# GLA layer of a two-block kernel: the gate's low-rank products stacked into one pass and moved, identity transposes put at the start, weight splits and boundary steps put in another order

## The chip, the cores and the metric

One core of a Trainium2 chip. The time is the device time of one launch in microseconds (us), the median of several runs. The profile is one more execution, recorded by the hardware profiler.

## What is computed

Two blocks run one after the other on x [256, 1024]. The first has a GLA mixer, a feed-forward (FFN), an attention mixer and a second FFN; the second has a recurrent mixer (`lru`) and a short-convolution mixer (`sc`). The change lies in the GLA mixer and in the steps between layers. Cut to what matters:

```python
h = rmsnorm(x, norm_mix[0])
proj = h @ w_in                                  # q, k: 512 columns each; v, g: 1024 each; r: 32
q, k, v, g, r = jnp.split(proj, [...], axis=-1)
r_f, r_b = jnp.split(r, 2, axis=-1)              # 16 columns a direction
def log_decay(r_dir, w_up, b_up):                # w_up [16, 512]
    return log_sigmoid(r_dir @ w_up + b_up) / 16.0
la_f, la_b = log_decay(r_f, ...), log_decay(r_b, ...)
o = gla_chunked(q, k, v, la_f, strict=False) + flip(gla_chunked(flip(q), flip(k), flip(v), flip(la_b), strict=True))
x = x + (rmsnorm(o, gla_norm) * silu(g)) @ w_out
x = x + conv_ffn(rmsnorm(x, norm_ffn[0]), ...)   # then attention, a second FFN, and the second block
```

## The kernel before

It is written engine by engine: each of the five engines has its own program, in a fixed order, and waits on semaphores. Nothing reorders anything, so an instruction that waits holds all that stands behind it on its engine.

**Weights** come as a stream of units of 128x2048 f32 (1 MB). SyncE loads unit u into one of three raw buffers; ScalarE writes its rounded high part `w_hi` (`split(u)`, L426); VectorE subtracts to get the low part `w_lo` (`split(u)`, L732), which also frees the raw buffer, so that SyncE may load unit u+3. High and low parts live in rings of six slots. A product of full precision is three passes of TensorE in the f32r format: high by high, high by low, low by high. Units 0 and 1 are q, 2 and 3 k, 4 to 7 v, 8 to 11 g, 12 to 15 the output projection, 16 on the FFN. `wide` (L1277) makes a turned result [columns, 256 positions], 48 matmuls of 256 columns a unit; `tall` (L1290) a result [positions, 1024] in `acc`, 24 matmuls of 512 columns a unit.

**Start.** x is loaded in two tiles of 128 positions. ScalarE squares and sums, GpSimd makes `rstd`, VectorE scales (`xn`, L740), TensorE turns `xn` by transposes against `ident` (L1224, eight of 128x128 a tile), which GpSimd makes after three other fills. Out of the turned tiles come `h_hi` (for the first half of tile 0 on VectorE, `front`, L746; for the other 12 blocks on ScalarE, `high`, L441) and `h_lo` (`low`, L758, eight on VectorE).

**The gate.** `wr` [1024, 32] is split into `wr_hi` and `wr_lo`, and 24 matmuls give r turned in 32 rows (L1319). VectorE copies them to `rt` (L820). After q and k, TensorE multiplies `gup` [32, 2, 512] by `rt` in plain f32, eight matmuls of 256 columns on 32 rows (L1330) into four ring banks; this is z. ScalarE takes |z + b| (L488), an exponential and a logarithm, VectorE min(z + b, 0) (L861), a subtraction (L871) and eight scans (L875). `differences`, the exponentials and `products` of a head follow (L884, L892 to L904), and TensorE's `scores(0)` waits for them. Between k and `scores(0)` TensorE has v (`project(U_V)`). VectorE also works out the constants `lam` of the recurrent mixer there (L824 to L845, some 25 tiny operations).

**The turn and the FFN behind it.** The GLA output is normed, turned (`turn`), and multiplied by units 12 to 15, tile 0 whole and then tile 1. When tile 0 is done, `residual(…, 0)` adds it to x, and x is normed and turned for `ffn0`, while TensorE is at tile 1; then the same for tile 1. VectorE's and ScalarE's splits 16 to 20 stand between these steps.

**Boundaries** ahead of `mix1`, `ffn1`, `lru` and `sc`: four halves of `residual` (L784), the sums of squares on ScalarE, the norm, the turn. VectorE norms the first half of tile 0 ahead of the last residual half.

Of the kernel before, what the change touches and what calls it, by code (L numbers as in the profile page):

```python
# [9 lines left out]
P = 128  # L10
D = 1024
S = 256
# [55 lines left out]
def generations():  # L68
# [3 lines left out]
    stages = [("rank", 1, 1), ("q", 2, 0), ("k", 2, 0), ("z", 4, 4),  # L72
# [51 lines left out]
HI = 1 + KC  # L124
LO = KC
N_CONSTS = 3
# [30 lines left out]
def two_block_kernel(nc, x_in, stream, par_in, row_in, wr_in, gup_in, gatew_in, rope_in, out):  # L157
# [4 lines left out]
    with ctx:  # L162
# [22 lines left out]
        gup = put("gup", [2 * GLA_RANK, 2, GLA_KEYS])  # L185
# [5 lines left out]
        rt = put("rt", [2 * GLA_RANK, S])  # L191
# [24 lines left out]
        wr_hi = put("wr_hi", [P, KC, 2 * GLA_RANK], f32r, at=stage_at)  # L216
        wr_lo = put("wr_lo", [P, KC, 2 * GLA_RANK], f32r, at=stage_at + 4 * KC * 2 * GLA_RANK)
# [33 lines left out]
        half_added = sem("half_added")  # L251
        wr_hi_ready, wr_lo_ready = sem("wr_hi_ready"), sem("wr_lo_ready")
# [10 lines left out]
        xn_ready = sem("xn_ready")  # L263
        x_turned = sem("x_turned")
# [5 lines left out]
        tables_ready = sem("tables_ready")  # L270
        z_abs, soft_ready, scan_ready = sem("z_abs"), sem("soft_ready"), sem("scan_ready")
# [31 lines left out]

        block = ctx.enter_context(nc.Block())
# [3 lines left out]
        def _(sp):  # L308
# [35 lines left out]
        def _(pool):  # L344
            own = Chain(pool, pool_own)
            own.mark(nc.gpsimd.memset(power[:, :], -0.5))
            for b in (ident, causal, chunk_on):
                own.mark(nc.gpsimd.memset(b[:, :] if b is not causal else b[:, :, :], 1.0))
            own.wait()
            nc.gpsimd.affine_select(out=ident[:, :], in_=ident[:, :], compare_op=ALU.is_equal, fill=0.0,  # L350
                                    base=0, pattern=[[-1, P]], channel_multiplier=1).then_inc(made, 1)
            nc.gpsimd.affine_select(out=causal[:, :, :], in_=causal[:, :, :], compare_op=ALU.is_ge, fill=0.0,
# [64 lines left out]
        def _(act):  # L417
# [10 lines left out]
            def sums(t, name):  # L428

                for half in range(2):  # L430
# [38 lines left out]
            nc.scalar.activation(wr_hi[:, :, :], wr[:, :, :], ACT.Copy).then_inc(wr_hi_ready, 1)  # L469
            turned0("mix0")  # L470
            turned1("mix0")
            split(0)
            split(1)

            own.mark(nc.scalar.activation(lam_p[:, :], par[:, C_LAM:C_LAM + LRU_HEADS], ACT.Abs))
            own.wait()
            nc.scalar.activation(lam_e[:, :], lam_p[:, :], ACT.Exp, scale=-1.0).then_inc(lam_ready, 1)
            for u in range(2, 6):
                split(u)

            for d in range(2):
                for b in range(2):
                    g = GEN["z"] + 2 * d + b
                    act.wait_ge(filled, FULL["z"] + 2 * d + b)
                    for k in range(2):
                        h = 2 * b + k
                        c = C_GB + GLA_HEADS * d + h
                        last = nc.scalar.activation(lt[:, d, h, :], ring[:, g % 4, k * S:(k + 1) * S], ACT.Abs,  # L488
                                                    bias=par[:, c:c + 1])
                        own.mark(last) if k == 0 else last.then_inc(z_abs, 1)  # L490
                split(6 + d)
# [7 lines left out]
            split(8)  # L499
# [18 lines left out]
            split(13)  # L518
            split(14)
# [3 lines left out]
            split(15)  # L523
# [8 lines left out]
            turned0("turn")  # L532
            turned1("turn")
            split(16)
            split(17)
# [189 lines left out]
        def _(dve):  # L725
# [9 lines left out]
            def normed(name, t, half):  # L735

                if half == 0:
                    dve.wait_ge(rms_ready, RMS[name] + t + 1)
# [3 lines left out]
            def front(name):  # L742

                c = C_GAMMA[name]
                dve.wait_ge(x_turned, HALVES * NTH[name] + 1)
                nc.vector.tensor_tensor(h_hi[:, 0:4, 0:P], turned_at(name, 0, 0, 4).rearrange("p (k s) -> p k s", k=4),  # L746
# [953 lines left out]
```

## Time and profile before

| | |
|---|---|
| median of 3 runs | 928.17 us (925.98 to 928.79) |
| the profiled execution, its own time | 925.22 us |
| its span | 923.5 us |
| TensorE matmuls | 880.2 us busy, 95% of the span |
| VectorE, ScalarE, GpSimd | 628.6, 500.8, 34.2 us busy |
| mean granted TensorE clock | 0.986 |

The span is what the trace covers; the time of the same execution is 1.7 us longer. The granted clock is TensorE's, as a share of 2.4 GHz, so 0.50 is 1.2 GHz. A busy time counts overlapping instructions once.

### The profile page before, as it was taken

Reading aid. Unit: us, or ns where it says so; the run is one execution under the profiler, and the core shown is the slowest. Engines: PE = TensorE matmul, PEld = TensorE weight load, DVE = VectorE, ACT = ScalarE, POOL = GpSimd, SP = SyncE. Lnnn points to the kernel's source line nnn. Section 1 sums busy time; section 2 is a strip of 40 time slices with the busy share of each in tenths; the row PEclk is TensorE's granted clock in tenths of the full one; section 3 lists DMA queues with packets and bytes.
Section 4 is the critical chain, followed back from the end, with each engine's and each line's share of the span. In section 5 each row is a group of like instructions: output and inputs, shape, how many; then the busy total and the mean of one; then the engine's idle time right before and its main releaser. Section 6 shows DMA issues by size and latency. Waiting matters only on the chain.

```text
span 923.5 us, 15067 instructions
## 1 busy us (share of the span) xinstructions
PE 880.2 (95%) x5804; PEld 802.6 (87%) x5804; DVE 628.6 (68%) x849; ACT 500.8 (54%) x675; POOL 34.2 (4%) x76
## 2 busy tenths in 40 slices
PE   6999988999999999799999999999999899999996
PEld 5988778999999977577999999979999789999995
DVE  5798656867667678766776676758877675654643
ACT  6466454645555453465564544548988674353431
POOL 2000100000000022101000000000000000000001
PEclk9999998999999999799999999999999999999999
DMA  8443433564554515135555355336264035545421
GB/s 321 174 162 137 182 137 137 185 227 144 219 182 165 215 48 210 46 137 178 210 202 208 136 222 187 143 131 229 97 227 178 24 125 218 204 159 205 166 85 45
DMA packets 22346, 152.52 MB, mean 165 GB/s; under 512 B 2496, under 2 KB 2624, under 8 KB 5024
## 3 DMA queue, kind: packets, MB, share of 16 engines
q1 hardware_dynamic: 21936, 149.45, 44.0%
q0 software_dynamic: 368, 2.49, 0.7%
q8 instruction: 29, 0.48, 0.2%
q14 instruction: 13, 0.11, 0.0%
HBM read 150.88 MB, written 1.05 MB: 165 GB/s over the span
## 4 chain that ended last, share of the span: by engine, by line
PE 85%; DVE 6%; ACT 5%; POOL 1%; issue 1%; DMA 0%; POOLq 0%; ACTq 0%; DVEq 0%
PE ring L1277 49%; PE acc L1290 26%; PE ring L1255 2%; DVE w_lo L732 1%; ACT xn L435 1%; PE acc L1224 1%; PE ring L1537 1%; PE acc L1452 1%; PE ring L1261 1%; PE ring L1488 1%; DVE x L784 1%; PE acc L1512 1%; ACT w_hi L426 1%; ACT h_hi L441 1%; POOL rstd L375 1%
## 5 line engine op out<-in xcount | busy, mean ns | idle before, releaser
L732 DVE TENSOR_TENSOR w_lo<-raw,w_hi 128x2048 fp32r<-128x2048 f32 (+1 forms) x146 | 317.7, 2199 | 101.9 <-ACT w_hi L426 101.7
L1277 PE MATMUL ring<-h_hi,w_hi 128*128 128x256 f32 x1280 | 363.5, 284 | 0.1
L1277 PE MATMUL ring<-h_hi,w_lo 128*128 128x256 f32 x1280 | 362.4, 283 | 0.0
L1277 PE MATMUL ring<-h_lo,w_hi 128*128 128x256 f32 x1280 | 362.4, 283 | 0.0
L426 ACT ACTIVATE w_hi<-raw 128x2048 fp32r<-128x2048 f32 (+1 forms) x146 | 264.2, 1841 | 14.2 <-DMA raw<-in_stream_dram 12.8
L1277 PEld LDWEIGHTS ring<-h_hi,w_hi 128*128 128x128 f32 x1280 | 243.9, 191 | 1.7 <-DVE w_lo L732 0.3
L1277 PEld LDWEIGHTS ring<-h_lo,w_hi 128*128 128x128 f32 x1280 | 243.9, 191 | 1.5
L1277 PEld LDWEIGHTS ring<-h_hi,w_lo 128*128 128x128 f32 x1280 | 243.9, 191 | 0.0
L972 DVE SCALAR_TENSOR_TENSOR cacc<-ring,par,cacc 128x255 f32<-128x255 f32 x176 | 76.9, 478 | 51.3 <-ACT cacc L546 46.3
L1290 PE MATMUL acc<-w_hi,a_hi 128*128 128x512 f32 x272 | 107.8, 396 | 3.9 <-DVE a_lo L1149 2.6
L1290 PE MATMUL acc<-w_hi,a_lo 128*128 128x512 f32 x272 | 107.5, 395 | 0.0
L1290 PE MATMUL acc<-w_lo,a_hi 128*128 128x512 f32 x272 | 107.0, 393 | 0.0
L546 ACT ACTIVATE cacc<-ring,par 128x256 f32<-128x256 f32 x88 | 44.9, 559 | 104.5 <-PE ring L1277 98.5
L1290 PEld LDWEIGHTS acc<-w_hi,a_hi 128*128 128x128 f32 x272 | 51.5, 189 | 15.3 <-DVE a_lo L1149 3.0
L1290 PEld LDWEIGHTS acc<-w_hi,a_lo 128*128 128x128 f32 x272 | 51.5, 189 | 11.2
L1290 PEld LDWEIGHTS acc<-w_lo,a_hi 128*128 128x128 f32 x272 | 51.5, 189 | 10.1
L1290 PE MATMUL acc<-w_hi,h_hi 128*128 128x512 f32 x128 | 51.3, 400 | 1.6 <-DVE h_lo L1083 0.9
L1290 PE MATMUL acc<-w_hi,h_lo 128*128 128x512 f32 x128 | 50.3, 393 | 0.0
L1290 PE MATMUL acc<-w_lo,h_hi 128*128 128x512 f32 x128 | 50.3, 393 | 0.0
L556 ACT ACTIVATE sgl<-cacc 128x512 f32<-128x512 f32 x22 | 13.9, 632 | 47.6 <-DVE cacc L972 47.6
L696 ACT ACTIVATE sgs<-ring 128x256 f32<-128x256 f32 x12 | 4.6, 384 | 62.2 <-PE ring L1277 62.2
L435 ACT ACTIVATE xn<-x 128x512 f32<-128x512 f32 x28 | 17.6, 629 | 33.9 <-DVE x L784 31.8
(205 smaller groups left out, 858.5 us busy)
## 6 DMA issues: line engine op xcount, KB each, us to landing
raw<-in_stream_dram SPq DMA_DIRECT2D x134, 1024.0 KB, 4.8
raw<-in_stream_dram SPq DMA_DIRECT2D x12, 512.0 KB, 5.2
gatew<-in_gatew_dram POOLq DMA_DIRECT2D x1, 1536.0 KB, 6.9
x<-in_x_dram SPq DMA_DIRECT2D x2, 512.0 KB, 3.8
out_dram<-xn SPq DMA_DIRECT2D x2, 512.0 KB, 2.6
row<-in_row_dram POOLq DMA_DIRECT2D x1, 640.0 KB, 8.7
par<-in_par_dram SPq DMA_DIRECT2D x1, 274.0 KB, 4.5
rope<-in_rope_dram POOLq DMA_DIRECT2D x1, 256.0 KB, 8.5
```

The costliest lines, as they stand in the source:

```text
L375: nc.gpsimd.tensor_tensor(rstd[:, t:t + 1], mean[:, t:t + 1], power[:, t:t + 1], ALU.pow).then_inc(rms_ready, 1)
L426: nc.scalar.activation(w_hi[:, u % RING, 0:n], raw[:, u % RAW, 0:n], ACT.Copy).then_inc(hi_split, 1)
L435: nc.scalar.activation(xn[:, t, at], x[:, t, at], ACT.Square, scale=D ** -0.5, accum_out=stat[:, 2 * t + half:2 * t + half + 1]).then_inc( ...
L441: return nc.scalar.activation(h_hi[:, kc, t * P:(t + 1) * P], turned_at(name, t, kc), ACT.Copy, scale=par[:, c:c + 1])
L546: last = nc.scalar.activation(cacc[:, k, half, :], ring[:, (G + 2 * e + k) % 4, half * S:(half + 1) * S], ACT.Identity, scale=par[:, bass. ...
L556: nc.scalar.activation(sgl[:, :, :], cacc[:, :, 1, :], ACT.Silu).then_inc(gate_ready, 1)
L732: nc.vector.tensor_tensor(w_lo[:, u % RING, 0:n], raw[:, u % RAW, 0:n], w_hi[:, u % RING, 0:n].bitcast(f32), ALU.subtract).then_inc(lo_spl ...
L784: nc.vector.tensor_tensor(x[:, t, at], acc[:, t, at], x[:, t, at], ALU.add).then_inc((half_added, acc_free[t])[half], 1)
L972: last = nc.vector.scalar_tensor_tensor(out=cacc[:, k, half, out_at], in0=ring[:, bank, lo + in_at.start:lo + in_at.stop], scalar=par[:, b ...
L1255: nc.tensor.matmul(ring[:, b, f * S:(f + 1) * S], w_parts[a][:, u % RING, lo:lo + P], h_hi[:, kc, :], start=kc == 0 and f == 0 and a == 0, ...
L1277: last = nc.tensor.matmul(ring[:, b, f * S:(f + 1) * S], w_parts[a][:, slot, lo:lo + P], h_parts[c][:, kc, :], start=kc == 0 and n == 0, s ...
L1290: last = nc.tensor.matmul(acc[:, t, half * 512:(half + 1) * 512], lhs(a, kc, t), w_parts[c][:, slot, j * D + half * 512:j * D + (half + 1) ...
```

## The change

1. GpSimd makes `ident` first, and TensorE multiplies it by itself 36 times (`WARM`) while x loads.
2. `wr_hi` and `wr_lo` hold three copies of the 32 columns, so that the 24 gate matmuls give r in 96 rows. `rt` gets rows 0 to 31 high, 32 to 63 low, 64 to 95 high; `gup` is loaded three times (behind unit 0), and holds high, high, low. Eight f32r matmuls on 96 rows then give all three parts of z at once. They stand behind the second q unit and write to `acc`; v waits for `z_read`. The first q unit is `first_wide`.
3. In the start VectorE makes the first half of `h_hi` of both tiles, and ScalarE eight blocks.
4. Evictions of q and k, splits and `lam` stand in another order; splits 16 and 17 are made ahead of and within the turn, and TensorE turns tile 0 for `ffn0` one unit earlier.
5. At the four boundaries ScalarE norms the first half of tile 0 (`xn_front`), and VectorE makes the last two residual halves back to back.

```diff
@@ constants @@
-HI = 1 + KC
+HI = {n: (1 + KC) * i - (KC // 2 if i else 0) for i, n in enumerate(NORMS)}
+WARM = 36
-N_CONSTS = 3
+N_CONSTS = 2
+COPIES = 3
+RANKS = COPIES * 2 * GLA_RANK
@@ sync @@
-            sp.dma_start(gup[:, :, :], gup_in.rearrange("r (a n) -> r a n", a=2)).then_inc(consts_loaded, 16)
-            for u in range(RAW):
-                load(u)
+            load(0)
+            for c in range(COPIES):
+                sp.dma_start(gup_raw[c * 2 * GLA_RANK:(c + 1) * 2 * GLA_RANK, :, :],
+                             gup_in.rearrange("r (a n) -> r a n", a=2)).then_inc(gup_loaded, 16)
+            load(1)
+            load(2)
@@ scalar: boundary @@
-                for t in range(T):
-                    sums(t, name)
+                sums(0, name)
+                sums(1, name, (0,))
+                act.wait_ge(rms_ready, RMS[name] + 1)
+                act.wait_ge(sumsq, SUMS[name] + 1)
+                nc.scalar.activation(xn[:, 0, 0:512], x[:, 0, 0:512], ACT.Copy, scale=rstd[:, 0:1]).then_inc(xn_front, 1)
+                sums(1, name, (1,))
@@ scalar: around the turn @@
-            split(15)
+            split(16)
...
             turned0("turn")
+            split(17)
             turned1("turn")
-            split(16)
-            split(17)
@@ vector: boundary @@
-                residual(layer, units, 1, (0,))
-                normed(name, 0, 0)
-                residual(layer, units, 1, (1,))
+                residual(layer, units, 1)
@@ vector: start @@
-            front("mix0")
+            for t in range(T):
+                front("mix0", t)
             low("mix0")
             split(0)
             split(1)
             dve.wait_ge(filled, FULL["rank"])
-            nc.vector.tensor_copy(rt[:, :], ring[0:2 * GLA_RANK, GEN["rank"] % 4, 0:S]).then_inc(ring_free, 1)
+            lower = slice(2 * GLA_RANK, 4 * GLA_RANK)
+            own.mark(nc.vector.tensor_copy(rt[:, :], ring[0:RANKS, GEN["rank"] % 4, 0:S]))
+            own.wait()
+            nc.vector.tensor_tensor(rt[lower, :], ring[lower, GEN["rank"] % 4, 0:S], rt[lower, :].bitcast(f32),
+                                    ALU.subtract).then_inc(ring_free, 1)
+            dve.wait_ge(gup_hi_ready, 1)
+            lower = slice(4 * GLA_RANK, RANKS)
+            nc.vector.tensor_tensor(gup[lower, :, :], gup_raw[lower, :, :], gup[lower, :, :].bitcast(f32),
+                                    ALU.subtract).then_inc(gup_ready, 1)
@@ tensor @@
-            pe.wait_ge(made, 3)
+            pe.wait_ge(made, 1)
+            for _ in range(WARM):
+                nc.tensor.transpose(ring[:, 3, 0:P], ident[:, :], ident[:, :])
...
-            for u, g in ((U_Q, GEN["q"]), (U_Q + 1, GEN["q"] + 1), (U_K, GEN["k"]), (U_K + 1, GEN["k"] + 1)):
-                wide(u, g % 4, g=g)
-            for d in range(2):
-                for b in range(2):
...
+            for n in range(4):
+                if n == 0:
+                    first_wide("mix0", U_Q, GEN["q"] % 4)
+                else:
+                    wide(U_Q + n, (GEN["q"] + n) % 4, g=GEN["q"] + n)
+                if n == 1:
+                    pe.wait_ge(gup_ready, 1)
+                    for d in range(2):
+                        for h in range(GLA_HEADS):
+                            last = nc.tensor.matmul(z_of(d, h), gup[:, d, h * P:(h + 1) * P], rt[:, :],
+                                                    start=True, stop=True, skip_group_check=True)
...
+            pe.wait_ge(z_read, 4)
             project(U_V)
...
-                    if (t, n) == (1, 3):
+                    if (t, n) == (1, 2):
                         turn("ffn0", 0)
```

TensorE's program from the gate to v, before (L1277 k's last unit, L1330 z, L1290 v's first):

```order
L1277 MATMUL ring<-h_lo,w_hi 128x256
L1277 MATMUL ring<-h_hi,w_lo 128x256
L1330 MATMUL ring<-rt,gup 128x256 x8
L1290 MATMUL acc<-w_hi,h_hi 128x512
L1290 MATMUL acc<-w_lo,h_hi 128x512
```

and in the change, where L1368 is the 36 identity transposes, L1280 the turn of x, L1379 the gate products, L1335 the q and k units and L1391 z:

```order
L1368 MATMUL ring<-ident 128x128 x36
L1280 MATMUL acc<-ident,xn 128x128 x16
L1379 MATMUL ring<-h_hi,wr_hi 96x256
...
L1335 MATMUL ring<-h_lo,w_hi 128x256
L1335 MATMUL ring<-h_hi,w_lo 128x256
L1391 MATMUL acc<-rt,gup 128x256 x8
L1335 MATMUL ring<-h_hi,w_hi 128x256
```

z has moved from behind k to between the second q unit and the first k unit, and its matmuls now write to `acc`.

VectorE's program from the second q eviction to the first `products` (L892, in the change L936), before (L732 is a split, `qT` and `kT` are evictions of q and k, L861 reads z):

```order
L848 TENSOR_SCALAR qT<-ring 128x512 x2
L732 TENSOR_TENSOR w_lo<-raw,w_hi 128x2048
L853 COPY kT<-ring 128x512 x2
L732 TENSOR_TENSOR w_lo<-raw,w_hi 128x2048
L861 TENSOR_SCALAR la<-ring,par 128x256 x4
L732 TENSOR_TENSOR w_lo<-raw,w_hi 128x2048
L861 TENSOR_SCALAR la<-ring,par 128x256 x4
L732 TENSOR_TENSOR w_lo<-raw,w_hi 128x2048
L871 TENSOR_TENSOR lt<-la,lt 128x1024
L875 SCALAR_TENSOR_TENSOR la<-chunk_on,lt 128x256 x4
L884 TENSOR_TENSOR dd<-la 128x256 x2
L732 TENSOR_TENSOR w_lo<-raw,w_hi 128x2048
```

and in the change (L761 is a split):

```order
L863 TENSOR_SCALAR qT<-ring 128x512
L879 TENSOR_SCALAR la<-acc,par 128x256 x8
L867 COPY kT<-ring 128x512
L761 TENSOR_TENSOR w_lo<-raw,w_hi 128x2048
L884 TENSOR_SCALAR lam_q<-lam_e 128x12
...
L761 TENSOR_TENSOR w_lo<-raw,w_hi 128x2048
L867 COPY kT<-ring 128x512
L761 TENSOR_TENSOR w_lo<-raw,w_hi 128x2048
L915 TENSOR_TENSOR lt<-la,lt 128x1024
L919 SCALAR_TENSOR_TENSOR la<-chunk_on,lt 128x256 x4
L761 TENSOR_TENSOR w_lo<-raw,w_hi 128x2048
```

The reading of z (`la`) now stands ahead of the k evictions and of splits 4 to 8, `lam` (the first of its rows is L884) behind split 4, and split 7 behind the scans.

VectorE's program around the turn, before (L938 norms the GLA output, L771 is `low_of`, L784 `residual`, L740 the norm of x):

```order
L771 SCALAR_TENSOR_TENSOR h_lo<-ring,par,h_hi 128x128 x4
L938 SCALAR_TENSOR_TENSOR xn<-acc,rstd,sg 128x256 x4
L771 SCALAR_TENSOR_TENSOR h_lo<-ring,par,h_hi 128x128 x12
L732 TENSOR_TENSOR w_lo<-raw,w_hi 128x2048 x2
L784 TENSOR_TENSOR x<-acc,x 128x512 x2
L740 TENSOR_SCALAR xn<-x,rstd 128x512 x2
L732 TENSOR_TENSOR w_lo<-raw,w_hi 128x2048
L746 TENSOR_TENSOR h_hi<-acc,par 128x4x128
L732 TENSOR_TENSOR w_lo<-raw,w_hi 128x2048
L784 TENSOR_TENSOR x<-acc,x 128x512 x2
```

and in the change (L984, L801, L814, L768 are the same four):

```order
L801 SCALAR_TENSOR_TENSOR h_lo<-ring,par,h_hi 128x128 x4
L984 SCALAR_TENSOR_TENSOR xn<-acc,rstd,sg 128x256 x4
L801 SCALAR_TENSOR_TENSOR h_lo<-ring,par,h_hi 128x128 x4
L761 TENSOR_TENSOR w_lo<-raw,w_hi 128x2048
L801 SCALAR_TENSOR_TENSOR h_lo<-ring,par,h_hi 128x128 x8
L814 TENSOR_TENSOR x<-acc,x 128x512 x2
L768 TENSOR_SCALAR xn<-x,rstd 128x512 x2
L761 TENSOR_TENSOR w_lo<-raw,w_hi 128x2048
L774 TENSOR_TENSOR h_hi<-acc,par 128x4x128
L761 TENSOR_TENSOR w_lo<-raw,w_hi 128x2048
L814 TENSOR_TENSOR x<-acc,x 128x512 x2
```

The two splits 16 and 17 that stood between the last `low_of` and `residual` are gone from there: one stands ahead of the turn, one between the `low_of` steps. Splits 18 and 19 keep their places.

## Rows read from the trace of the kernel before

**Rows 1.** The page: chain by engine; ScalarE's split (count, busy us, mean ns, idle before).
```profile
PE 85%; DVE 6%; ACT 5%; POOL 1%; issue 1%; DMA 0%; POOLq 0%; ACTq 0%; DVEq 0%
...
L426 ACT ACTIVATE w_hi<-raw 128x2048 fp32r<-128x2048 f32 (+1 forms) x146 | 264.2, 1841 | 14.2 <-DMA raw<-in_stream_dram 12.8
```

**Rows 2.** The chain that ended last, 0 to 152 us: start, us, what.
```profile
17.02 23.29 PE ring L1277 x192
...
40.31 3.93 PE ring L1330 x16
...
44.24 23.26 PE acc L1290 x96
...
70.65 5.45 PE acc L1290 x24
...
79.26 5.47 PE acc L1290 x24
```

**Rows 3.** Timeline of TensorE, 7 to 17.5 us: start, us, what [idle before <-releaser].
```profile
7.29 3.65 PE L1224 MATMUL acc<-ident,xn 128*128 128x128 f32 x16 [7.29 <-DVE xn L740]
...
12.17 0.39 PE L1319 MATMUL ring<-h_hi,wr_hi 128*32 128x256 f32 x1 [1.23 <-DVE h_lo L758]
...
15.99 0.40 PE L1319 MATMUL ring<-h_hi,wr_hi 128*32 128x256 f32 x1
...
16.57 0.28 PE L1319 MATMUL ring<-h_lo,wr_hi 128*32 128x256 f32 x1
```

**Rows 4.** Timeline of GpSimd, the identity.
```profile
1.63 0.29 POOL L350 TENSOR_SCALAR_AFFINE_SELECT ident<-ident 128x128 f32<-128x128 f32 x1
```

**Rows 5.** Timeline of VectorE, 0 to 110 us.
```profile
8.88 0.42 DVE L814 TENSOR_TENSOR wr_lo<-wr,wr_hi 128x256 fp32r<-128x256 f32 x1
...
11.54 3.23 DVE L758 SCALAR_TENSOR_TENSOR h_lo<-acc,par,h_hi 128x256 fp32r<-128x256 f32 x8 [1.65 <-ACT h_hi L441]
...
14.69 4.48 DVE L732 TENSOR_TENSOR w_lo<-raw,w_hi 128x2048 fp32r<-128x2048 f32 x2
...
26.24 0.17 DVE L824 TENSOR_SCALAR lam_q<-lam_e 128x12 f32<-128x12 f32 x1
...
31.02 0.17 DVE L845 TENSOR_SCALAR sp<-lam_p 128x12 f32<-128x12 f32 x1
...
52.52 1.23 DVE L871 TENSOR_TENSOR lt<-la,lt 128x1024 f32<-128x1024 f32 x1 [1.52 <-ACT lt L498]
...
60.05 0.76 DVE L884 TENSOR_TENSOR dd<-la 128x256 f32<-128x256 f32 x2
...
65.82 0.19 DVE L904 COPY qt<-qd 128x64 f32<-128x64 f32 x1
...
78.66 0.42 DVE L911 COPY qT<-ring 128x256 f32<-128x256 f32 x1 [1.53 <-PE ring L1350]
```

**Rows 6.** Windows: length, PE busy (xmatmuls), granted clock, DMA share, GB/s.
```profile
44.00:47.00 3.00, 3.00 (x8) 0.51 0.82 276
...
142.00:146.00 4.00, 3.72 (x18) 0.51 0.27 111
...
425.63:429.70 4.07, 2.41 (x16) 1.00 0.16 24
```

**Rows 7.** Timelines of VectorE (two rows) and TensorE (one), 136 to 142 us.
```profile
136.45 2.29 DVE L732 TENSOR_TENSOR w_lo<-raw,w_hi 128x2048 fp32r<-128x2048 f32 x1 [2.71 <-ACT w_hi L426]
...
138.66 1.28 DVE L784 TENSOR_TENSOR x<-acc,x 128x512 f32<-128x512 f32 x2
...
142.28 1.97 PE L1224 MATMUL acc<-ident,xn 128*128 128x128 f32 x8 [6.11 <-DVE xn L740]
```

**Rows 8.** Timelines of VectorE and TensorE, 425 to 426 us.
```profile
425.49 0.68 DVE L784 TENSOR_TENSOR x<-acc,x 128x512 f32<-128x512 f32 x1
...
425.63 0.66 PE L1224 MATMUL acc<-ident,xn 128*128 128x128 f32 x4 [0.46 <-DVE xn L740]
```

**Rows 9.** DMA issues, 0 to 30 us: count, size, us from issue to landing.
```profile
gup<-in_gup_dram SPq DMA_DIRECT2D x1, 128.0 KB, 5.1
```

More of the change, by code:

```diff
@@ L184, in two_block_kernel @@
         wr = put("wr", [P, KC, 2 * GLA_RANK])
-        gup = put("gup", [2 * GLA_RANK, 2, GLA_KEYS])
+        gup = put("gup", [RANKS, 2, GLA_KEYS], f32r)
         rope = put("rope", [P, T, 2, HD])
@@ L190, in two_block_kernel @@
         power = put("power", [P, 20])
-        rt = put("rt", [2 * GLA_RANK, S])
+        rt = put("rt", [RANKS, S], f32r)
         half_mean = put("half_mean", [P, T])
@@ L345, in _ @@
             own = Chain(pool, pool_own)
-            own.mark(nc.gpsimd.memset(power[:, :], -0.5))
-            for b in (ident, causal, chunk_on):
-                own.mark(nc.gpsimd.memset(b[:, :] if b is not causal else b[:, :, :], 1.0))
+            own.mark(nc.gpsimd.memset(ident[:, :], 1.0))
             own.wait()
@@ L426, in split, with sums @@
                 nc.scalar.activation(w_hi[:, u % RING, 0:n], raw[:, u % RAW, 0:n], ACT.Copy).then_inc(hi_split, 1)
-            def sums(t, name):
-                for half in range(2):
+            def sums(t, name, halves=(0, 1)):
+                for half in halves:
                     if name != "mix0":
@@ L477, in _ @@
             nc.scalar.activation(lam_e[:, :], lam_p[:, :], ACT.Exp, scale=-1.0).then_inc(lam_ready, 1)
-            for u in range(2, 6):
-                split(u)
+            split(2)
+            split(3)
             for d in range(2):
                 for b in range(2):
-                    g = GEN["z"] + 2 * d + b
                     act.wait_ge(filled, FULL["z"] + 2 * d + b)
@@ L498, in _ @@
                 nc.scalar.activation(lt[:, d, :, :], lt[:, d, :, :], ACT.Ln, bias=1.0).then_inc(soft_ready, 1)
-            split(8)
+            for u in range(5, 9):
+                split(u)
             def exps(h):
@@ L517, in _ @@
                 split(9 + h)
-            split(13)
-            split(14)
+            for u in range(13, 16):
+                split(u)
             act.wait_ge(used, U_G + 4)
@@ L845, in _ @@
             nc.vector.tensor_scalar(sp4[:, :], lam_p[:, :], LRU_C / 2, None, ALU.mult).then_inc(sp4_ready, 1)
[L846 to L864 removed]
+            split(5)
+            evicted(3)
+            split(6)
             dve.wait_ge(made, 3)
@@ L928, in _ @@
                 split(9 + h)
+            split(13)
             scores(GLA_HEADS - 1)
-            for u in range(13, 16):
+            for u in range(14, 17):
                 split(u)
@@ L944, in _ @@
                     low_of("turn", 0, 0)
-            for t, b in ((0, 1), (1, 0), (1, 1)):
-                low_of("turn", t, b)
-            split(16)
+            low_of("turn", 0, 1)
             split(17)
+            for b in range(2):
+                low_of("turn", 1, b)
             residual(1, U_GO + 4, 0)
@@ L1217, in bank, with xn_at_turn @@
                     pe.wait_ge(ring_free, g - 3 + 4 * i)
+            def xn_at_turn(name):
+                split_here = ("mix1", "ffn1", "lru", "sc")
+                by_act = split_here.index(name) + 1 if name in split_here else 0
+                return HALVES * NTH[name] - max(by_act - 1, 0), by_act
             def turn(name, t):
```

125 lines of the change are left out of this document (74 added, 51 removed).

## The prediction

> **What bounds the kernel.** I read the page first: TensorE is busy for 95% of the span (the table), and 85% of the chain that ended last is its own [rows 1]. So a gain has to come out of TensorE's work, its clock or its few waits; time saved on another engine counts only where TensorE waits for it. Then I went along the chain through the first 152 us, which is where most of the change lies [rows 2]. TensorE runs without a pause from 17.02 us to the end of v at 67.50 (44.24 + 23.26): four q and k units in 23.29, z in 3.93, v in 23.26. What decides when it starts is VectorE, which makes `h_lo` and then the low part of unit 0 until about 16.9 [rows 5]. Behind that, the windows show the granted clock at 0.51 over 44 to 47 and again over 142 to 146 [rows 6], and the timeline a pause of 6.11 us until 142.28, in which VectorE runs split 19 first (136.45) and only then the residual of tile 1 (138.66) [rows 7]. The rest is untouched but for the four boundaries.
>
> **z in one f32r pass.** Before: eight plain f32 matmuls, 3.93 us [rows 2]. An f32r matmul of 256 columns takes 23.29 / 192 = 0.121 us [rows 2], whatever rows it uses (I take that from the gate product, which fills 32 columns and goes at a like pace, below), so eight take 0.97. Gain 2.96. Right behind z before, the clock stands at 1.2 GHz for v's first matmuls: 0.51 over 44 to 47 [rows 6], after four microseconds in which TensorE only had products on 32 rows. v took 23.26 where four units at 5.45 [rows 2] are 21.80. With z at 1 us between two full units I expect no fall: gain 1.46. Both ends for this: 0 if the clock falls anyway, 1.46 if not; I take 1.46, since nothing else stands between q and v.
>
> **The start.** VectorE's list from 8.88: `wr_lo` has 768 columns instead of 256, and no row has that size. 512 columns of such a step took 0.68 [rows 8] and 1024 took 1.23 [rows 5], so about 0.96 and 0.88 to the next start (ends overlap the next start by some 0.08). Two `front` steps of 512 columns follow, 0.61 from start to start: 8.88 + 0.88 + 0.61 + 0.61 = 10.98 for the first `h_lo`, against 11.54 before, which had waited 1.65 for ScalarE's blocks [rows 5]. Everything behind shifts by 0.56: `w_lo` of unit 0 at 16.3, q at 16.46. This needs the turn of x in time. `ident` was ready at 1.92 behind three other fills [rows 4]; without them I put it at 1.4. In the gate products 18 starts took 15.99 − 12.17 = 3.82 us, 0.212 each, then 4 took 0.58, 0.145 and falling [rows 3]: 256 columns in 0.212 is the 1.2 GHz level, 0.121 the 2.4 level, and the rise came some 4 us in. The x transposes went at 3.65 / 16 = 0.23 [rows 3]. So 36 warm ones cost 36 × 0.212 = 7.6 us at the low level, and about 6 if the clock rises after 4 (19 low, 17 at half that): TensorE is free at 7.4 to 9.0, x was there at 7.29. With the rise the turn ends by 9.4, in time for both fronts. The 36 cost nothing then: they lie in the 7.29 us in which TensorE waits for x [rows 3]. Gain 0.56 (bounds: −0.9, below, and 0.6).
>
> **Does TensorE or VectorE set `scores(0)` then?** TensorE: q and k units of 23.29 / 4 = 5.82. The first k unit ends at 16.46 + 3 × 5.82 + 0.97 = 34.9, v at 34.9 + 5.82 + 21.80 = 62.5. VectorE waits in order for that k unit (third eviction), so its list restarts at 34.9: eviction 0.6 (512 columns again), split 4 2.2 (two took 4.48), `lam` 31.02 + 0.1 − 26.24 = 4.9, split 5 2.2, eviction 0.6, split 6 2.2, the subtractions and scans 60.05 − 52.52 = 7.5, split 7 2.2, and differences, split 8 and products 65.82 + 0.19 − 60.05 = 6.0 [rows 5]. That is 28.4, so 63.3. The reading of z (eight steps of 256 columns, some 0.4 each, from about 29) hides under the first k unit, and its exponentials on ScalarE under `lam`. So VectorE is last by 0.8 us: `scores(0)` starts at 63.3 instead of 67.50. **Gain 4.2 of the 5.0 that TensorE alone would give.** Behind it a head takes 79.26 − 70.65 = 8.6 us on TensorE [rows 2], and VectorE waits 1.53 us of it for the scores [rows 5], so it catches up and the 4.2 stays.
>
> **The splits at the turn.** Call E the end of tile 1's last unit, 142.28 − 6.11 = 136.17 [rows 7]. Before, the second residual half began at 138.66 + 0.6, E + 3.1. Split 19 was late since ScalarE did it behind the blocks of tile 0 for `ffn0`, whose turn stood one unit before E. Now the turn stands two units before (12 × 5.45 / 24 = 2.7 us earlier [rows 2]), units 18 and 19 load long before (splits 16 and 17 no longer hold their raw buffers), and the first residual isn't queued behind two splits. ScalarE (a split is 1.84 [rows 1], and its split 19 ended at 136.4, E + 0.2, before): that end moves from E + 0.2 to E − 2.5; VectorE's split 19 until E − 0.3, residual halves at E − 0.3 and E + 0.3. **Gain 2.8.** Bounds: 0 if split 19 stays ahead of the residual as late as now, 3.1 if nothing does. The splits moved ahead lie in VectorE's waits between the heads and in its wait for the tile 1 blocks. The 0.51 clock after the pause [rows 6] costs up to 4 × 0.5 = 2 us; the pause shrinks from 6.1 to 3.3 us, and I count nothing for it.
>
> **The boundaries.** At `ffn1` VectorE began the last residual half at 425.49, behind the norm of the first half, and TensorE had ended at 425.63 − 0.46 = 425.17 [rows 8]: 0.3 to win. Elsewhere the residual waits for TensorE's end anyhow: 0.1 or nothing, and in `mix1` ScalarE hands over its half 0.1 later. Together 0.3, bounds −0.4 and 0.8.
>
> **Sum.** 4.2 + 2.8 + 0.3 = 7.3 us: from the profiled execution's 925.2 to 917.9. The median of the runs shown is 3 us above it, so against 928.17 I predict 920.9.
>
> **Rivals.**
> 1. *The identity transposes don't raise the clock.* For it: they multiply a matrix of ones and zeros by itself. Against: between 425.63 and 429.70 TensorE had 16 transposes and nothing else, busy 2.41 of 4.07 us, and the clock stayed at 1.00 [rows 6]. Then the 36 end at 9.0, the x turn at 9.0 + 3.65 = 12.7, the second front at 11.8, q starts at 17.9, 0.9 late instead of 0.56 early: gain 5.8, 922.4. The Trainium skill speaks for it ("TensorE: Matmul & The Clock Gate", Part 4): transpose mode isn't counted as TensorE being busy, and the full clock doesn't engage. By that rule the warm-up only costs; by the window just named, transposes at least hold the clock. Chance 0.15.
> 2. *The pauses undo the warm-up*: TensorE idles about 2 us before the gate products and 2 us before q, so q may start at 1.2 GHz. Four low microseconds cost 2: gain 5.3, 922.9. Chance 0.12.
> 3. *One of the two big terms stays out*: split 19 is late for a cause that I miss (4.5, 923.7), or VectorE's list of 28.4 us grows, as each raw buffer is freed later (3.1, 925.1). Chance 0.12.
> 4. *Slower: the three copies of `gup` hold unit 1.* They stand ahead of it in the queue, 128 KB that took 5.1 us from issue to landing [rows 9]. If they go one behind the other instead of beside each other, unit 1 comes up to 15 us later than now (an estimate from that row); q's second unit needs its split at 22.3, and its two split steps take 4.1, so it has to land by 18.2. If it lands 10 us behind that, 7.3 won become 2.7 lost: 930.9. It decides from 7.3 us behind that. Against: three times 128 KB are a little over a third of a unit. Chance 0.04.
> 5. *More*: the clock stays up at `ffn0` too, 1.8 us more, 919.1. Chance 0.07.
>
> **Numbers.** The forecast itself has 0.50. A measurement of this kernel tells 0.3%, 2.8 us, from no change. All cases but rival 4 and the low end of rival 3 gain more: faster 0.87, same 0.09, slower 0.04. The range goes from rival 5 with 2.5 us of run-to-run spread, as the three runs show, to rival 3: 916.5 to 925.
>
> **What would show it.** Right: z about 1 us, with the clock at 1.00 over v's start; first matmul of q at 16.3 to 16.6 at 0.12 us; `scores(0)` near 63.3 with VectorE as its releaser; second residual half within 0.5 us of E; pause before `ffn0` near 3.3. Wrong: x transposes starting after 8.5 or at 0.21; q at 0.21; splits waiting for DMA between 13 and 25 us; a pause of 6 us still.

## The result and the profile after

The changed kernel takes 920.61 us in the median against 927.92 for the kernel before, 7 runs each. Two of its seven were disturbed and far longer; the other five lie between 918.97 and 921.24, and the ratio goes by them: 0.9926, 95% interval 0.9905 to 0.9946. By the medians that is 7.3 us faster. The profiled execution took 921.24, with a span of 919.5 us, so between the two profiles only 4.0 us of the 7.3 are seen; where the other 3 went is told at the end of this section.

The page of the changed kernel, its chain by engine and ScalarE's split (before: [rows 1]):

```profile
PE 81%; DVE 7%; ACT 5%; issue 1%; POOL 1%; POOLq 0%; ACTq 0%; DVEq 0%
...
L448 ACT ACTIVATE w_hi<-raw 128x2048 fp32r<-128x2048 f32 (+1 forms) x146 | 264.3, 1839 | 25.4 <-DMA raw<-in_stream_dram 21.8
```

TensorE's share of the chain fell from 85% to 81%, but that is mostly not a gain. The shares of the changed kernel add up to 95%, because its chain can be followed back only to 50.28 us; before, the stretch from 17.02 to 50.28 counted for TensorE, some 33 us or 3.6% of the span. What did change is who stands last ahead of `scores(0)`: from 50.28 to 63.48 the chain now runs over VectorE.

The timeline of TensorE, 0 to 29 us (start, us, what; before: [rows 3]):

```profile
1.43 6.82 PE L1368 MATMUL ring<-ident 128*128 128x128 f32 x36 [1.43 <-POOL ident L368]
8.09 1.91 PE L1280 MATMUL acc<-ident,xn 128*128 128x128 f32 x16
11.71 0.33 PE L1379 MATMUL ring<-h_hi,wr_hi 128*96 128x256 f32 x1 [1.71 <-DVE h_lo L788]
...
14.73 0.28 PE L1379 MATMUL ring<-h_hi,wr_lo 128*96 128x256 f32 x1
16.56 0.39 PE L1313 MATMUL ring<-h_hi,w_hi 128*128 128x256 f32 x1 [1.55 <-DVE w_lo L761]
16.78 0.28 PE L1313 MATMUL ring<-h_hi,w_lo 128*128 128x256 f32 x1
...
28.18 1.11 PE L1391 MATMUL acc<-rt,gup 96*128 96x256 f32 x8
```

The first row is the 36 identity transposes, the second the turn of x at 1.91 / 16 = 0.12 us each instead of 0.23. The gate products go from start to start in 0.12 to 0.17 instead of 0.21, and q begins at 16.56 instead of 17.02. z is the last row: 1.11 us, and it stands between q and k instead of behind both.

Windows of the same kernel (length, busy us of each engine, then the granted clock behind them; before: [rows 6]):

```profile
6.00:7.00 1.00, 1.00 (x7) 1.00 (x6) 0.33 (x1) 1.00 (x5) 0.83 (x3) 1.00 1.13 450
7.00:8.00 1.00, 1.00 (x12) 1.00 (x11) 0.56 (x2) 0.60 (x1) 0.92 (x3) 1.00 0.94 385
...
40.00:50.00 10.00, 10.00 (x49) 8.38 (x49) 9.52 (x22) 4.18 (x3) 0.00 (x0) 1.00 0.57 214
...
137.00:140.00 3.00, 3.00 (x15) 2.94 (x15) 2.18 (x6) 3.00 (x8) 0.00 (x0) 0.50 0.03 5
```

The number behind an x counts the matmuls that ran in the window, with those already under way at its edges: seven transposes between 6 and 7 us, twelve between 7 and 8. From start to start the transposes go in 0.21 us until 7.0 and in 0.11 behind it, so the pace changes at about 7.0. (The clock column reads 1.00 there all along, also where the pace is that of 1.2 GHz; at the start of the trace the pace is the better witness.) Over 40 to 50, where v now begins, the clock is 1.00; before, v began at 44.24, and it was 0.51 over 44 to 47. Behind the turn at `ffn0` it is still low, 0.50 over 137 to 140.

VectorE's timeline to 64 us (before: [rows 5]):

```profile
8.89 0.95 DVE L842 TENSOR_TENSOR wr_lo<-wr,wr_hi 128x768 fp32r<-128x768 f32 x1
9.76 1.28 DVE L774 TENSOR_TENSOR h_hi<-acc,par 128x512 fp32r<-128x512 f32 x2
11.08 3.23 DVE L788 SCALAR_TENSOR_TENSOR h_lo<-acc,par,h_hi 128x256 fp32r<-128x256 f32 x8
14.22 4.49 DVE L761 TENSOR_TENSOR w_lo<-raw,w_hi 128x2048 fp32r<-128x2048 f32 x2
...
35.09 0.69 DVE L867 COPY kT<-ring 128x512 f32<-128x512 f32 x1 [2.37 <-PE ring L1335]
...
37.89 0.17 DVE L884 TENSOR_SCALAR lam_q<-lam_e 128x12 f32<-128x12 f32 x1
...
42.75 2.29 DVE L761 TENSOR_TENSOR w_lo<-raw,w_hi 128x2048 fp32r<-128x2048 f32 x1
```

and the chain that ended last, from the end of VectorE's products for head 0 (before: [rows 2]):

```profile
63.32 0.11 DVE qt L948
...
63.48 0.49 PE ring L1405 x2
...
66.89 5.49 PE acc L1348 x24
...
75.54 5.48 PE acc L1348 x24
...
130.05 2.29 DVE w_lo L761
132.34 0.61 DVE x L814
...
132.98 1.34 ACT xn L457 x4
...
135.34 0.50 DVE xn L768
...
135.88 1.27 PE acc L1280 x8
137.15 5.32 PE ring L1313 x32
```

VectorE waits for the first k unit until 35.09, then has 28.4 us of work without a wait, and `scores(0)` begins at 63.48 behind VectorE's last product. The first `o` unit begins at 66.89 instead of 70.65, 3.8 us earlier; the second at 75.54 instead of 79.26, 3.7 earlier. At the turn the split (130.05) ends just when TensorE does (132.5), the residual follows at once, and the turn is at 135.88 instead of 142.28: 6.4 us won by then.

Of these 6.4 the profiled execution kept 4.0. Two windows tell why. The kernel before, 600 to 630 and 720 to 750 us (length, TensorE busy, granted clock):

```profile
600.00:630.00 30.00, 27.84 (x182) 1.00 0.30 109
720.00:750.00 30.00, 25.60 (x136) 0.94 0.06 18
```

and the changed one:

```profile
600.00:630.00 30.00, 27.84 (x174) 0.94 0.30 106
720.00:750.00 30.00, 25.49 (x147) 0.89 0.21 73
```

From TensorE's end to the turn of tile 1 it is 3.05 to 3.16 us at `lru` and at `sc` in both kernels; the clock is lower there in the changed one. From the low products of `ffn1` to those of `lru` it took 193.3 us against 192.2, and from there to `sc` 122.6 against 121.4. Nothing of the change acts there but the order of the boundary steps, so this had to be tested.

### The profile page after: what moved, and what is told of

Same layout as the page of the kernel before. It is cut to its first block, busy times and chain, and to the rows that moved or that the text cites. A ratio compares the mean times of both kernels' runs of the same rounds, so it can differ in the third digit from the quotient of the medians.

```text
span 919.5 us, 15132 instructions
## 1 busy us (share of the span) xinstructions
PE 881.4 (96%) x5832; PEld 806.4 (88%) x5832; DVE 630.4 (69%) x848; ACT 504.2 (55%) x676; POOL 34.3 (4%) x76
## 4 chain that ended last, share of the span: by engine, by line
PE 81%; DVE 7%; ACT 5%; issue 1%; POOL 1%; POOLq 0%; ACTq 0%; DVEq 0%
PE ring L1335 47%; PE acc L1348 24%; PE ring L1313 2%; DVE w_lo L761 2%; PE acc L1515 1%; PE ring L1600 1%; PE acc L1280 1%; PE ring L1319 1%; PE ring L1551 1%; ACT xn L457 1%; PE acc L1575 1%; ACT w_hi L448 1%; DVE x L814 0%; ACT pm L647 0%; DVE cacc L1018 0%
## 5 line engine op out<-in xcount | busy, mean ns | idle before, releaser
L761 DVE TENSOR_TENSOR w_lo<-raw,w_hi 128x2048 fp32r<-128x2048 f32 (+1 forms) x146 | 317.8, 2199 | 101.1 <-ACT w_hi L448 100.9
L1335 PE MATMUL ring<-h_hi,w_hi 128*128 128x256 f32 x1264 | 358.6, 284 | 0.0
L1335 PE MATMUL ring<-h_hi,w_lo 128*128 128x256 f32 x1264 | 357.7, 283 | 0.0
L1335 PE MATMUL ring<-h_lo,w_hi 128*128 128x256 f32 x1264 | 357.6, 283 | 0.0
L1335 PEld LDWEIGHTS ring<-h_lo,w_hi 128*128 128x128 f32 x1264 | 240.7, 190 | 1.5
L1335 PEld LDWEIGHTS ring<-h_hi,w_hi 128*128 128x128 f32 x1264 | 240.7, 190 | 1.4
L1335 PEld LDWEIGHTS ring<-h_hi,w_lo 128*128 128x128 f32 x1264 | 240.7, 190 | 0.0
```

Of the source, the lines that this page charges most:

```text
L761: nc.vector.tensor_tensor(w_lo[:, u % RING, 0:n], raw[:, u % RAW, 0:n], w_hi[:, u % RING, 0:n].bitcast(f32), ALU.subtract).then_inc(lo_spl ...
L1335: last = nc.tensor.matmul(ring[:, b, f * S:(f + 1) * S], w_parts[a][:, slot, lo:lo + P], h_parts[c][:, kc, :], start=kc == 0 and n == 0, s ...
```

## The experiments

Each kernel is the changed one with the edit shown. The kernel before ran beside them: 927.61 us in the median for the first four, 928.11 for the next four, 926.53 for the last four.

**The warm-up alone.**

```diff
-WARM = 36
+WARM = 0
```

> The changed kernel without its 36 identity transposes. My theory: VectorE's list sets the start, so the warm-up is worth little. x is turned at 1.2 GHz (0.21 us a transpose) and the 24 gate products too, 24 x 0.212 = 5.1 us from 11.7; the first q matmul then starts at 16.8 to 17.1 instead of 16.56, at 0.12 us or soon so, and scores(0) at 63.7 to 64.0: 0.3 to 0.5 us of the 7.3. Rival: the warm-up carries the start. Then q starts after 17.5, or runs for microseconds at 0.21, and everything behind is 2 us or more late.

Measured: 921.02 (919.17 to 922.27, 5 runs), ratio 0.9936 (0.9915 to 0.9958). Its TensorE timeline:

```profile
7.41 3.65 PE L1280 MATMUL acc<-ident,xn 128*128 128x128 f32 x16 [7.41 <-DVE xn L768]
11.81 0.33 PE L1379 MATMUL ring<-h_hi,wr_hi 128*96 128x256 f32 x1 [0.75 <-DVE h_lo L788]
```

The turn of x takes 3.65 us again, but it ends at 11.06 and `h_lo` is there at 11.8 only, 0.1 later than with the warm-up. q begins at 16.66, `scores(0)` at 63.58: 0.1 us behind the changed kernel at both. But VectorE's first step, the norm of x, began 0.11 us later in this execution already (6.78 against 6.67), ahead of anything that the transposes touch. So no gain of the 36 transposes shows. What VectorE does between 8.9 and 16.5 sets the start of q, and it hardly needs a fast turn.

**The order of the boundary steps alone**, put back as before (the core):

```diff
-                sums(0, name)
-                sums(1, name, (0,))
...
+                for t in range(T):
+                    sums(t, name)
...
-                residual(layer, units, 1)
-                normed(name, 0, 1)
+                residual(layer, units, 1, (0,))
+                normed(name, 0, 0)
+                residual(layer, units, 1, (1,))
+                normed(name, 0, 1)
...
-                split_here = ("mix1", "ffn1", "lru", "sc")
+                split_here = ()
```

> The changed kernel with the four boundaries as before (VectorE norms the first half of tile 0 ahead of the last residual half). My theory: worth 0.3 us in all, most of it at ffn1. Rival: the low clock that the changed kernel's trace shows at the lru and sc boundaries (0.83 and 0.84 of their 10 us, 2.3 us lost against before) comes from the new order there. Then it is gone here: 1.00 over 610 to 620 and a time 2 us below the changed kernel's. If the fall is the chance of one execution, it will be there or not in these runs whatever the order.

Measured: 920.82 (919.26 to 921.19, 4 runs), ratio 0.9928 (0.9901 to 0.9955). From `ffn0` to `ffn1` its profile took 284.8 us (285.0 in the changed kernel, 284.9 in the one before). The single boundaries do differ. From TensorE's end to its first product behind the two turns it is 4.54 us at `ffn1` before the change and in this run, and 4.26 in the changed kernel, whose two waits there are:

```profile
419.93 1.09 PE L1280 MATMUL acc<-ident,xn 128*128 128x128 f32 x8 [0.79 <-ACT xn L485]
422.20 1.09 PE L1280 MATMUL acc<-ident,xn 128*128 128x128 f32 x8 [1.18 <-DVE xn L768]
```

At `mix1` it is 4.70 before and in this run, and 5.03 in the changed kernel: there ScalarE's half lets the first transposes begin 0.78 us behind TensorE's end instead of 0.30, and behind them TensorE waits 0.44 us more, for VectorE's `h_hi`. At `lru` it is 4.37 against 4.25 where the clock is up (second profile of the changed kernel), at `sc` 4.25 against 4.26 (the kernel before and the changed one). So 0.3 is won at `ffn1`, 0.3 lost at `mix1` and 0.1 won at `lru`; together that is nothing that the times can tell.

**The turn of tile 0 and the splits around it put back as before** (the core; the low splits on VectorE alike):

```diff
-            for u in range(13, 16):
+            for u in range(13, 15):
                 split(u)
...
             turned0("turn")
-            split(17)
             turned1("turn")
+            split(16)
+            split(17)
...
-                    if (t, n) == (1, 2):
+                    if (t, n) == (1, 3):
```

> The changed kernel with splits 15 to 17 and the turn for ffn0 where they stood before. Theory: TensorE's pause before the turn of tile 1 for ffn0 is 6.1 us again instead of 3.4, the second residual half starts about 3.1 us behind the end of the output projection instead of 0.4, and the time is 2.7 us above the changed kernel's. Rival: the pause hangs on what came before the turn (z, loads), and stays near 3.4.

Measured: 923.17 (922.16 to 924.14, 9 runs), ratio 0.9955 (0.9942 to 0.9968). The pause before the turn is 6.11 us again, as in [rows 7].

**Only the place of that turn**, one unit later, with all splits where the change has them:

```diff
-                    if (t, n) == (1, 2):
+                    if (t, n) == (1, 3):
```

> The changed kernel with only one thing undone there: TensorE turns tile 0 for ffn0 one unit later, as before, and the splits stay moved. Theory: split 19 stands behind the blocks of that turn on ScalarE, so it is late again by a unit, 2.7 us: pause near 6, time 2.4 to 2.7 us above the changed kernel's, the same as with all of it undone. Rival: moving splits 16 and 17 is what helps. Then the pause stays near 3.4 and only undoing the splits costs.

Measured: 922.76 (922.15 to 924.31, 9 runs), ratio 0.9954 (0.994 to 0.9969). ScalarE's, VectorE's and TensorE's timelines of this kernel, 129 to 139 us:

```profile
129.82 1.14 ACT L463 ACTIVATE h_hi<-acc,par 128x128 fp32r<-128x128 f32 x4 [4.34 <-PE acc L1280]
130.83 1.93 ACT L448 ACTIVATE w_hi<-raw 128x2048 fp32r<-128x2048 f32 x1
```
```profile
132.79 2.29 DVE L761 TENSOR_TENSOR w_lo<-raw,w_hi 128x2048 fp32r<-128x2048 f32 x1 [2.72 <-ACT w_hi L448]
135.00 1.28 DVE L814 TENSOR_TENSOR x<-acc,x 128x512 f32<-128x512 f32 x2
```
```profile
138.62 1.75 PE L1280 MATMUL acc<-ident,xn 128*128 128x128 f32 x7 [6.11 <-DVE xn L768]
```

One line gives back the whole 2.7 us at the turn (138.62 against 135.88) and 2.1 by the medians. ScalarE idles 4.34 us until the turn of tile 0 is there, evicts its blocks, and only then reaches split 19; VectorE waits for it until 132.79 and has the residual behind it. Moving the splits ahead changes nothing as long as split 19 stands behind that turn. The other half, the early turn with the splits where they were, was not run. With the old splits VectorE norms x of tile 0 at 126.41 only, and the early turn stands at 126.0; so the moved splits may save about 1 us there (an estimate from these two rows).

**z, taken apart.** In plain f32 on 32 rows, as before the change but in the new place (two runs), then as f32r on 96 rows issued four times, and as f32r on 32 rows four times:

```diff
-                            last = nc.tensor.matmul(z_of(d, h), gup[:, d, h * P:(h + 1) * P], rt[:, :],
+                            last = nc.tensor.matmul(z_of(d, h), gup_raw[0:32, d, h * P:(h + 1) * P], rt[0:32, :].bitcast(f32),
```
```diff
+                            for _ in range(4):
                                 last = nc.tensor.matmul(z_of(d, h), gup[:, d, h * P:(h + 1) * P], rt[:, :],
```
```diff
+                            for _ in range(4):
+                                last = nc.tensor.matmul(z_of(d, h), gup[0:32, d, h * P:(h + 1) * P], rt[0:32, :],
```

> The changed kernel with z as before in plain f32 on 32 rows, at its new place (it leaves out the low part of r, and VectorE reads z only when all of it is there). z takes 3.93 us. Theory: TensorE's clock falls behind a stretch of products on 32 rows, wherever it stands: 0.5 for some 3 us over the first k unit, which starts 3 us later and takes 1.2 to 1.5 us longer. Rival: it fell before for another cause of that place, and stays at 1.00 here.

> The changed kernel with each z matmul made four times (the result is the same), 32 of 0.12 us, so z also takes 3.9 us, on 96 rows. Theory: the rows in use count, so the clock stays at 1.00. Rival: it is the length of the stretch, or the gaps in it, that counts; then it falls to 0.5 as in the run on 32 rows in plain f32.

> The changed kernel with z on rows 0 to 31 alone, in f32r, each matmul four times: 3.9 us again (it leaves out the two low products). Theory, rows count: the clock falls as in plain f32 on 32 rows. Rival, the form counts: plain f32 lets it fall and f32r doesn't, so it stays at 1.00.

> The changed kernel with z in plain f32 on 32 rows, a second look. In the kernel before, 3.9 us of such products were followed by a clock of 0.51 over 44 to 47; in the first look of this kernel, 3.7 us of them were followed by 1.00. If the fall is a matter of the execution, this look may show either; if it depends on the place and the work around, 1.00 again. Time 923.8 where the clock stays up, some 1.5 us more where it falls.

Measured, one time each: 923.84 and 922.96 for plain f32, 923.93 for 96 rows four times, 925.14 for 32 rows four times. z and the window from 32 to 36 us in plain f32 (first run), in 96 rows, and in 32 rows of f32r:

```profile
28.12 3.72 PE L1392 MATMUL acc<-rt,gup_raw 32*128 32x256 f32 x16
...
32.00:36.00 4.00, 4.00 (x35) 1.00 0.02 4
```
```profile
28.16 3.99 PE L1392 MATMUL acc<-rt,gup 96*128 96x256 f32 x32
...
32.00:36.00 4.00, 4.00 (x36) 1.00 0.00 0
```
```profile
28.22 5.14 PE L1392 MATMUL acc<-rt,gup 32*128 32x256 f32 x32
...
32.00:36.00 4.00, 4.00 (x19) 0.50 0.00 0
```

With z at 3.72 to 3.99 us instead of 1.11, `scores(0)` begins at 66.21, 66.34 and (plain f32 again) 66.21 instead of 63.48, and the times, of one run each, are 2.3 to 3.5 us above the changed kernel's medians (920.61, and 919.43 beside the last of them): what a slower z costs reaches the end. (In the plain f32 form VectorE also waits for all of z before it reads the first part.) So z's products gave the gain that the prediction counted. On the clock the answer is partly open. 96 rows kept it at 1.00; with 32 rows of f32r it fell within z, at about 31, which is why z took 5.14, and brought `scores(0)` to 69.63, 3.3 us behind the 66.34 of the 96 rows. Plain f32 on 32 rows kept 1.00 in both runs, against the expectation for the first of them; the kernel before had 0.51 over 44 to 47 after the same products [rows 6]. z stood elsewhere there (behind both q and k units, not between them), and I can't say whether the place decides or the chance of an execution; so how much of the 1.46 us belongs to the new format and how much to the new place stays open.

**VectorE's `lam` steps earlier**, all of them from the wait for `lam_ready` to `sp`, ahead of the third eviction, where VectorE waited 2.37 us for TensorE at 35.09:

```diff
+            dve.wait_ge(lam_ready, 1)
...
             evicted(2)
             split(4)
-            dve.wait_ge(lam_ready, 1)
...
```

> The changed kernel with VectorE's lam steps moved from behind split 4 to ahead of the third eviction, where VectorE waits 2.4 us. Theory: VectorE's list sets scores(0) by 0.8 us. lam (4.9 us) then lies half in that wait, the list behind the first k unit shrinks by about 2.3 us, VectorE is no longer last, v's fourth unit isn't held up (0.46 us pause at 57.5 gone) and scores(0) starts at 62.5 to 62.7 instead of 63.48: 0.8 us faster. Rival: TensorE then waits for split 4 at the start of v, and nothing or less is won.

Measured: 919.28 (918.47 to 919.38, 4 runs), ratio 0.991 (0.9889 to 0.9931). `scores(0)` begins at 62.36, right at the end of v's last product (62.13, 0.23 from start to start), the turn at 134.60 instead of 135.88. VectorE was what `scores(0)` waited for, and without it TensorE alone gives 1.1 us more. The trace tells this and the medians don't: 919.28 is 1.3 us below the first median of the changed kernel and 0.2 below its second (919.43, further down), and the intervals overlap.

**The pauses before the turns filled** with identity transposes into a free bank, 24 at `ffn0` and 9 each at `ffn1`, `lru` and `sc`; then the same together with the early `lam` steps:

```diff
+            def keep(bank_at, n):
+                for _ in range(n):
+                    nc.tensor.transpose(ring[:, bank_at, 0:P], ident[:, :], ident[:, :])
...
-                turn(f"ffn{n}", 1)
                 bank(G)
+                keep(G % 4, 9 if n else 24)
+                turn(f"ffn{n}", 1)
```

> The changed kernel with identity transposes into a free bank while TensorE waits for the last turn: 24 at ffn0 (about 2.6 us of its 3.39 us pause at 0.11 each), 9 each at ffn1, lru and sc (1 us). Theory: the clock is low for some 4 us after a turn because TensorE did little in the pause before it, so with the pause filled it stays at 1.00: the high group of ffn0 behind the turn at 0.12 instead of 0.21 to 0.33 a product, 1.5 to 1.8 us won there, and up to 1 us each at lru and sc, where the clock fell in some profiles: median 917 to 919.5. Rival: what lowers the clock is not the pause but the few columns of the turn's own mix, and the clock still reads 0.5 for 3 to 4 us after the turn: 920.6 as before, or 0.1 to 0.5 more where the transposes delay the turn.

> The same filling together with the lam steps of VectorE moved ahead of the third eviction (which gave 1.1 us at scores(0) by itself, 919.3). Theory: the two gains lie in different stages and add: scores(0) near 62.4, clock 1.00 behind the turn of ffn0, median 916 to 918. Rival as for the filling alone: 919.3.

> The changed kernel once more, on the same chip as the two kernels with the pauses filled, for a direct comparison: 920.6 within 1 us. Its profile tells whether the low clock at lru and sc (1.1 and 0.9 us lost against the kernel before in its first profile) belongs to the kernel or to the execution: theory, to the execution, since two kernels that differ little showed 1.00 there: L1313 at lru 4.07 or 4.70 by chance.

Measured on one chip: pauses filled 915.77 (915.12 to 917.01, 4 runs), ratio 0.9885 (0.9859 to 0.9911); with `lam` early 915.11 (915.05 to 915.91, 4 runs), ratio 0.9876 (0.985 to 0.9902); the changed kernel again 919.43 (918.43 to 921.09, 6 runs), ratio 0.9924 (0.9904 to 0.9945). TensorE's timeline with the pauses filled, and a window behind the turn:

```profile
132.18 2.78 PE L1274 MATMUL ring<-ident 128*128 128x128 f32 x24
135.73 1.09 PE L1285 MATMUL acc<-ident,xn 128*128 128x128 f32 x8 [0.77 <-DVE xn L768]
136.94 0.36 PE L1318 MATMUL ring<-h_hi,w_hi 128*128 128x256 f32 x1
...
138.00:141.00 3.00, 3.00 (x28) 1.00 0.00 0
```

and the same window of the changed kernel run beside it:

```profile
138.00:141.00 3.00, 3.00 (x16) 0.50 0.02 5
```

28 products ran in these 3 us instead of 16. The turn is hardly earlier (135.73 against 135.82): the gain at `ffn0` is clock. At its low products it is 1.6 us (140.84 against 142.43, of which 0.1 was there at the turn), to `ffn1` 0.8 more (284.0 against 284.8), to `lru` nothing (192.1 both, the clock was up in both), to `sc` 0.9 more (120.2 against 121.1); spans 913.4 and 916.7, together 3.3, and 3.7 by the medians. That is more than either expectation had (917 to 919.5, 916 to 918).

Not all of this belongs to the filled pauses. The 0.8 to `ffn1` lies ahead of the pause that was filled there: it is in the 276.6 us up to that turn, against 277.4, and behind the turn both kernels take 7.4. The kernel with both changes has the same filling and took 285.0 to `ffn1`. So this 0.8 is what the clock did in `mix1`, where nothing was filled. For `ffn0` and `sc` the profiles speak clearly: over 130 to 145 and over 720 to 750 the clock is under 1.00 in all twelve without the filling (the kernel before, and the changed one in its variants) and 1.00 in the two with it. Which of the filled pauses keeps it up at `sc` isn't shown, since 0.8 of the 0.9 is there before the turn for `sc` already.

The second profile of the changed kernel had 1.00 over 600 to 630 and took 192.1 us to `lru`, without the 1.1 us of its first profile. So that low stretch belongs to the execution and not to the change: the boundary kernel, the kernel without warm-up and this one showed 1.00 there; others with the very same code at that place 0.94.

The early `lam` steps gave 1.1 us alone and about 0.7 beside the filled pauses, the spans being 913.4 both. Where it went is in the chain of the two kernels. The one with the pauses filled:

```profile
373.03 1.21 ACT pm L647 x4
374.28 1.15 PE ring L1557 x4
375.45 0.70 DVE mx L1121
```

and with `lam` early too:

```profile
372.07 1.21 ACT pm L647 x4
373.33 2.09 PE ring L1557 x4
375.44 0.70 DVE mx L1121
```

The second is 0.95 us ahead until 373.33, in `mix1`'s attention; there four score products take 2.09 instead of 1.15, at a clock of 0.65 over 370 to 380 against 0.85, and the lead is gone at once. From the turn for `mix1` to the one for `ffn1` it is 92.9 us here and in the first profile of the changed kernel, and 91.9 with the pauses filled alone; so it is rather that one execution which was short there. Both kernels lose clock in this stage of small products and waits, and where in it the fall lands isn't the same.

## Why the prediction was right

The forecast was 920.9 us and the median came to 920.6; 7.3 us won, as the sum said. Term by term:

**The start**: 0.56 predicted, 0.46 measured (q at 16.56). VectorE's `wr_lo` took 0.95 for the estimated 0.96, and the first `h_lo` came at 11.08 for 10.98. But the warm-up, which the prediction wanted so that the turn of x is in time, was not needed: without it 0.36 remains, and the 0.1 between is the later start of VectorE in that execution. What won, by the rows, is that VectorE makes the first half of both tiles' `h_hi` itself and no longer waits 1.65 us for ScalarE's blocks [rows 5]; no run takes this out by itself. Rival 1, that the identity transposes don't raise the clock, fell: with nothing else on TensorE the transposes went from 0.21 us from start to start to 0.11 at about 7.0. The Trainium skill ("TensorE: Matmul & The Clock Gate", Part 4) has it that the full clock doesn't engage for transpose mode, which doesn't count as TensorE being busy in the same way. These rows speak against it, as far as the transposes here run in that mode (no row names it), and the filled pauses speak against it a second time. Rival 2, that the pauses behind the warm-up undo it, happened in part: in several of the profiles the gate products went at the low clock for some three microseconds (0.21 us from start to start instead of 0.13). It cost nothing, as VectorE's `w_lo` at 16.5 is later than TensorE either way.

**z**: 2.96 predicted as 3.93 to 0.97; its row says 1.11, and the next product starts 0.95 behind its first. Of the 3.93 some 0.2 was clock: at 1.00 the same products took 3.72. Four times that work delayed `scores(0)` by 2.9.

**The clock behind z**: 1.46 predicted, and it reads 1.00 over 40 to 60. As said above, no run tells how much of it the new format gave and how much the new place. A pause of 0.46 us stood in v's fourth unit, waiting for a split, which the sum didn't have; it was covered, since VectorE was later anyway.

**Which engine sets `scores(0)`**: VectorE, by 0.8, at 63.3 was predicted. It began at 63.48, 28.4 us after the first k unit's eviction as worked out (28.4), the unit itself 0.2 late. The early `lam` steps confirm the limit: 1.1 us more without it. That the 4.2 stay was nearly so: 4.0 at `scores(0)`, 3.8 at the first `o` unit (its first score product begins behind a wait, 0.49 against 0.22), 3.7 from the second on. This 0.5, 4.2 predicted and 3.7 measured, is the largest miss of a term.

**The turn**: 2.8 predicted, 2.7 measured (6.11 to 3.39), with the residual 0.2 before TensorE's end. The prediction named split 19 behind the blocks of tile 0 as the cause, and the place of the turn, the loading of units 18 and 19 and the residual's place in the queue as the means. Of the three the place of the turn was needed; the moved splits alone gave nothing, and whether the early turn needs them wasn't run.

**The boundaries**: 0.3 predicted, about 0.1 in the traces and nothing that the times can tell. The 0.3 at `ffn1` came (4.54 to 4.26 us). What the sum had too small is that ScalarE hands over its half later in `mix1`: 0.1 was allowed for, and it cost 0.3 (4.70 to 5.03), since VectorE's `h_hi` is later with it.

The terms measured in the trace make 3.7 + 2.7 = 6.4 us, and the medians 7.3. The 0.9 between them is within the spread of the medians (the intervals of the two comparisons with the changed code reach from 5.0 to 8.9 us), so the agreement to 0.3 us is luck; that each large term came out within 0.5 is not. What the sum missed for single executions is the clock: four runs of the changed kernel had spans of 917.2 at a mean granted clock of 0.988, 917.7 at 0.986, and 918.6 and 918.9 at 0.982 (the profiled one, 919.5 at 0.985, stands outside this row). Rival 5, that the clock stays up at `ffn0`, did not come by itself (0.50 over 137 to 140) but with the pause filled, and it is worth 1.5 us there, where the prediction priced it at 1.8.

## What to carry to other kernels

When a stage gets shorter on one engine, list the other engine's work in order from its last wait: here 28.4 us of VectorE's steps said to 0.2 us when the scores would start and which steps to move next. When a step is late, look for what it is queued behind on its own engine, and move that: one line that put a turn one unit earlier was worth 2.7 us at that place, and moved splits without it nothing. When TensorE has to wait ahead of dense work, spare transposes into a free bank can be worth as much as what shortens the wait: 51 of them won 3.7 us here by the medians, of which the traces show 1.5 at `ffn0` and 0.9 on the way to `sc`.

## What the runs showed of the hardware

- Identity transposes alone, 128 columns each, brought TensorE from 0.21 us from start to start to 0.11, 5.6 us after the first of them in one execution and about 3 us after it in two others (36 in 5.49 and 5.59 us instead of 6.82), and 24 of them kept the clock at 1.00 over a wait of 3.4 us that otherwise ended with 0.50 for some 3 us.
- The same code had its low stretches in different places in different executions (1.00 or 0.94 over 600 to 630), which made about 1 us each in the time. A difference between two profiles of that size is no effect of a change until a second profile shows it.
- In 32 f32r products of 256 columns on 32 rows the clock fell to 0.50 less than 3 us after the first; 32 on 96 rows kept 1.00, and 3.72 us of plain f32 on 32 rows kept it too. One profile each, and two of the last.
